# Pre-norm roots applied behind the projections, and attention one head deeper, in a hybrid decoder kernel

## The chip, the cores and the metric

One core of a Trainium2 chip runs the whole program. The metric is the device time of one execution in microseconds (us), lower is better. Engines are written as in the profile: PE (TensorE), DVE (VectorE), ACT (ScalarE), POOL (GpSimd), SP (the queue that issues most DMAs).

## The reference, cut to what matters

Tokens: T = 272 rows (16 learned meta tokens ahead of 256 real ones), model width 1024. Two layers.

```
layer 0: h += rms(rglru_block(rms(h, a_pre)), a_post)          # "ao" is the second norm
         h += rms(swiglu(rms(h, f_pre)), f_post)               # "f" is the first norm, "fo" the second
shared:  u = rms(h, kv_norm); ckv, k_rope = split(u @ w_dkv, [256])
         kv = rms(ckv, latent) @ w_ukv ; k_rope = rope(k_rope)
layer 1: cq = rms(rms(h, b_pre) @ w_dq, q_norm)                # kv_norm and b_pre share one root, "b"
         q = cq @ w_uq ; 16 heads: softmax(q k^T) v, causal, blocks of 128 queries
         h += rms(o @ w_o, b_post)                             # "bo"
         h += rms(moe_swiglu(rms(h, m_pre)), m_post)           # 8 experts, top 2
rms(x, g) = x * rsqrt(mean(x*x) + eps) * g
```

The root of a row is one number per token. It commutes with the matrix product over the features: rms(h, g) @ W = (h * g) @ W, each token's column then multiplied by its 1/root.

## The kernel before, in words

Activations lie transposed: a tile is 128 features by 272 tokens, and the residual hT has KD = 8 such blocks. Every product is formed from values split in two halves (hi is the rounded value, lo the rest), as three matmuls (`product`, L426 to L430): hi·hi, hi·lo, lo·hi. A tile of eight blocks is therefore 24 matmuls of 272 columns (`columns_tile`).

**Weights.** SP loads them in chunks of 128x2048 in the order of `PLAN`, RAW = 6 buffers deep. ACT rounds each to w_hi (L977), DVE subtracts to w_lo (L1331); both go to one of SPLIT = 3 buffers, so chunk n may only be rounded when PE has finished chunk n - 3. `ahead(n)` stands in ACT's and DVE's programs where they are to bring the chunks up to n.

**Tiles.** The PSUM tiles take six banks in the order of `tile_plan`; a tile's bank is free when its emptier, "A" (ACT) or "V" (DVE), has emptied the tile six places before. Banks 6 and 7 take the sums of squares.

**A norm** (`root`, `reciprocal_of_root`, `residual`, `squares`, `sum_taken`, `normalise`). For "ao" and "fo" ACT writes each emptied tile and its square, POOL adds six of the squares (`add_squares`, L890), PE multiplies by ones for the sum over partitions (L456, L449), ACT takes the root, DVE its reciprocal (1.85 us) and then, per block, scales mix (L1345) and adds it to hT (L1371). For the next norm, "f" or "b", ACT squares hT block by block (L997), PE sums all eight squares (L449, two matmul records each), ACT takes the root (L1004), DVE the reciprocal (L1340); then DVE writes the scaled block (L1345), ACT rounds it (L1011), DVE subtracts (L1359), and PE may use block k.

**Feed-forward.** 12 rounds j of gate tiles f_g and up tiles f_u, two each. ACT empties f_g with Silu, DVE multiplies f_u from PSUM by it into f_h; ACT and DVE split f_h into hid_hi and hid_lo. Then 8 f_down tiles.

**Latents.** PE runs ckv (2 tiles), krope (1), cq (3); ACT empties them with their squares; roots "ckv" and "cq"; then `ukv` gives keys and values: ACT empties kn and v tiles, POOL copies the rotary part of the keys to all heads (L907 to L909), fills `blank` with zeros and writes it out 34 times.

**Attention.** In PE's order, for head h: `scores(h)`; after heads 1, 5 and 9 the four tiles of the next group of queries; `turn_probs(h - LAG)` (transposes, L585); `weigh(h - LAG - 1)` (L595 to L598). DVE empties scores with the mask (L1562), ACT exponentiates (L1199), DVE divides (L1575), ACT copies the turned tile (L1211), and after heads 3, 7, 11 and 15 both split another weight chunk. LAG = 2. The output of each pair of heads is split by ACT (L1215) and DVE (L1583), and b_out (8 tiles) consumes it. The experts' loop follows.

Of the kernel before, what the change touches and what calls it, by code (L numbers as in the profile page):

```python
# [44 lines left out]
LAG = 2  # L45
# [22 lines left out]
def chunk_plan():  # L68
# [9 lines left out]
    plan += [("dkv", 0, KD * LORA), ("dkr", 0, KD * ROPE), ("dq", 0, KD * 256), ("dq", 1, KD * 128)]  # L78
# [9 lines left out]
EC = 4 * UT + KE // 2  # L88
assert EC % RAW == 0 and EC % SPLIT == 0

# [4 lines left out]
def tile_plan():  # L95
# [8 lines left out]
    for j in range(KF // 2):  # L104
        plan += [("f_g", 2 * j, "A"), ("f_g", 2 * j + 1, "A"), ("f_u", 2 * j, "V"), ("f_u", 2 * j + 1, "V")]
    plan += [("f_down", m, "A") for m in range(KD)] + [("ckv", m, "A") for m in range(KL)] + [("krope", 0, "V")]
    plan += [("cq", m, "A") for m in range(KQ)]
# [4 lines left out]
    plan += queries(0)  # L112
    for h in range(HEADS):
        plan += [("s", h, "V")]
        if h % 4 == 1 and h // 4 < 3:
            plan += queries(h // 4 + 1)
        if h >= LAG:
            plan += [("pt", h - LAG, "A")]
# [18 lines left out]
NORMED = {name: n - KD for name, n in PART.items()}  # L137
# [10 lines left out]
ADDED = {"ao": KD - 2, "fo": 2 * (KD - 2), "bo": 3 * (KD - 2)}  # L148
# [11 lines left out]
def pieces(name, k, src, dst):  # L160

    if name == "dkr":
        s = src[:, 0:k * ROPE].rearrange("p (k n) -> p k n", k=k)
        d = dst[:, 0:k * 3 * ROPE].rearrange("p (k n) -> p k n", k=k)
        h = ROPE // 2
        return [(d[:, :, 0:h], s[:, :, h:ROPE]), (d[:, :, h:ROPE], s[:, :, 0:h]),
# [20 lines left out]
def yoco_kernel(nc, w, params, consts, gain_rows, x_tok, out):  # L187
    with ExitStack() as ctx:
# [75 lines left out]
        s_sb = mix.rearrange("p k n -> p (k n)")[:, 0:3 * SW].rearrange("p (h n) -> p h n", h=3)  # L264
# [51 lines left out]
        sq_added = sem("sq_added")  # L316
        gated, gelu_done = sem("gated"), sem("gelu_done")
# [22 lines left out]
        nbias, rsum, rcp = (small[:, 112 + 16 * k:112 + 16 * k + 9] for k in range(3))  # L340
# [15 lines left out]
        def source(name, j):  # L356
# [10 lines left out]
                "dkr": lambda: w_dkv[:, :, LORA:LORA + ROPE],  # L367
                "dq": lambda: w_dq[:, :, 256 * j:min(256 * j + 256, QLORA)],
# [9 lines left out]
        def split_views(n, buf):  # L378
# [3 lines left out]
            cols = {"dkr": KD * 3 * ROPE, "uq": KQ * 512}.get(name, cols)  # L382
# [18 lines left out]
        def _(pe):  # L401
# [115 lines left out]
            pe.wait_ge(in_const, 16)  # L517
            sum_taken("f")
            for j in range(KF // 2):
                for name, key in (("f_g", "f_gate"), ("f_u", "f_up")):  # L520
                    wc = chunk(key, j)
                    for m in (2 * j, 2 * j + 1):
                        columns_tile(name, m, wc, P * (m % 2), u, KD, P, *([("chunk", CH[(key, j)])] if m % 2 else []),
                                     need="f" if (name, m) == ("f_g", 0) else None)
# [18 lines left out]

            sum_taken("b")
            wc = chunk("dkv", 0)
            for m in range(KL):
                columns_tile("ckv", m, wc, P * m, u, KD, P, *([("chunk", CH[("dkv", 0)])] if m else []),
                             need=None if m else "kv")
            columns_tile("krope", 0, chunk("dkr", 0), 0, u, KD, QK, ("chunk", CH[("dkr", 0)]))
            for m in range(KQ):  # L550
                columns_tile("cq", m, chunk("dq", m // 2), P * (m % 2), (ub_hi, ub_lo), KD, P,
                             *([("chunk", CH[("dq", m // 2)])] if m else []), need=None if m else "b", at=REAL)
                if m == 0:
                    for k in range(KL):
                        sum_emptied("ckv", "ckv", k, sq[:, k, :])
# [1249 lines left out]
```

## Time and profile before

| | |
|---|---|
| median of 3 runs | 1584.25 us (1583.27 to 1586.55) |
| the profiled execution's own time | 1584.72 us |
| its span, first to last instruction | 1582.9 us, so 1.8 us lie around it |
| PE busy | 1485.3 us (94%) |
| DVE busy | 1183.3 us (75%) |
| ACT busy | 1026.8 us (65%) |
| POOL busy | 95.6 us (6%) |
| mean granted TensorE clock | 0.976 of full |

Busy times of different engines overlap. PE's busy time counts a slow matmul as busy as a fast one, so the granted clock is to be read beside it.

### The profile page before, as it was taken

What the parts mean: (1) busy time and instruction counts of PE and PEld (TensorE: products, weight loads), DVE (VectorE), ACT (ScalarE), POOL (GpSimd) and SP (SyncE); (2) the same over time, 40 slices, a digit from 0 to 9 for tenths busy, and PEclk for the clock granted to TensorE, in tenths of its full rate; (3) what the DMA queues carried; (4) which work ended last, traced back from release to release, by engine and by line L of the source; (5) the groups of instructions that cost most, each with busy time, mean ns of one, the idle gap of its engine ahead of it and who ended that gap; (6) DMA issues with size and microseconds to landing.
All of it is one profiled execution on the core that took longest, in us unless ns stands there. A gap on an engine that the chain in (4) does not pass through costs nothing.

```text
span 1582.9 us, 21443 instructions
## 1 busy us (share of the span) xinstructions
PE 1485.3 (94%) x7852; PEld 1258.5 (80%) x7852; DVE 1183.3 (75%) x1089; ACT 1026.8 (65%) x1085; POOL 95.6 (6%) x112
## 2 busy tenths in 40 slices
PE   7787999997788879999999999999999999999997
PEld 6787999996676768877878878887887887887785
DVE  6685554535746278888888888888888888888987
ACT  6874444443565357777777767777767777767675
POOL 2001000000250110000000000000000000002500
PEclk9999999998899979999999999999999999999999
DMA  8345455542286259999999999999999999999993
GB/s 268 115 124 189 150 170 187 164 146 83 84 324 260 80 207 368 360 343 403 346 350 399 353 346 397 360 352 383 366 355 370 373 356 370 355 372 361 401 363 148
DMA packets 166704, 455.27 MB, mean 288 GB/s; under 512 B 8688, under 2 KB 77552, under 8 KB 152320
## 3 DMA queue, kind: packets, MB, share of 16 engines
q1 hardware_dynamic: 160432, 432.07, 75.5%
q0 software_dynamic: 6224, 22.55, 3.7%
q8 instruction: 32, 0.52, 0.1%
q14 instruction: 16, 0.13, 0.0%
HBM read 429.42 MB, written 25.17 MB: 287 GB/s over the span
## 4 chain that ended last, share of the span: by engine, by line
PE 84%; DVE 8%; ACT 4%; issue 3%; DMA 0%; DVEq 0%; SPq 0%; ACTq 0%
PE bank L428 26%; PE bank L430 26%; PE bank L429 26%; PE bank L698 2%; DVE w_lo L1593 1%; DVE w_lo L1331 1%; DVE x_lo L1683 1%; ACT w_hi L977 1%; ACT w_hi L1228 1%; PE bank L449 1%; DVE mix_sq L1345 1%; DVE rstd L1340 1%; PE bank L474 1%; PE bank L575 1%; PE bank L687 0%
## 5 line engine op out<-in xcount | busy, mean ns | idle before, releaser
L1593 DVE TENSOR_TENSOR w_lo<-raw,w_hi 128x2048 fp32r<-128x2048 f32 x338 | 774.4, 2302 | 139.8 <-ACT w_hi L1228 139.1
L1228 ACT CAST w_hi<-raw 128x2048 fp32r<-128x2048 f32 x338 | 645.6, 1916 | 261.7 <-PE bank L430 255.6
L428 PE MATMUL bank<-w_hi,x_hi 128*128 128x512 f32 x896 | 357.5, 399 | 3.6 <-DVE x_lo L1683 3.6
L429 PE MATMUL bank<-w_lo,x_hi 128*128 128x512 f32 x896 | 355.2, 396 | 0.0
L430 PE MATMUL bank<-w_hi,x_lo 128*128 128x512 f32 x896 | 354.9, 396 | 0.0
L1331 DVE TENSOR_TENSOR w_lo<-raw,w_hi 128x2048 fp32r<-128x2048 f32 (+8 forms) x93 | 153.1, 1669 | 163.7 <-ACT w_hi L977 163.6
L428 PE MATMUL bank<-u_hi,w_hi 128*128 128x272 f32 (+2 forms) x632 | 187.5, 297 | 19.1 <-DVE u_lo L1359 8.7
L428 PEld LDWEIGHTS bank<-w_hi,x_hi 128*128 128x128 f32 x896 | 169.0, 189 | 44.8 <-issue 3.8
L430 PEld LDWEIGHTS bank<-w_hi,x_lo 128*128 128x128 f32 x896 | 168.7, 188 | 41.2
L429 PEld LDWEIGHTS bank<-w_lo,x_hi 128*128 128x128 f32 x896 | 168.8, 188 | 39.5
L430 PE MATMUL bank<-u_hi,w_lo 128*128 128x272 f32 (+2 forms) x632 | 184.9, 293 | 0.0
L429 PE MATMUL bank<-u_lo,w_hi 128*128 128x272 f32 (+2 forms) x632 | 184.7, 292 | 0.0
L428 PE MATMUL bank<-w_hi,eh_hi 128*128 128x512 f32 x448 | 180.4, 403 | 1.3 <-DVE w_lo L1593 1.3
L430 PE MATMUL bank<-w_hi,eh_lo 128*128 128x512 f32 x448 | 177.6, 396 | 0.0
L429 PE MATMUL bank<-w_lo,eh_hi 128*128 128x512 f32 x448 | 177.4, 396 | 0.0
L977 ACT CAST w_hi<-raw 128x2048 fp32r<-128x2048 f32 (+8 forms) x93 | 124.9, 1372 | 65.2 <-PE bank L430 64.5
L428 PEld LDWEIGHTS bank<-u_hi,w_hi 128*128 128x128 f32 (+1 forms) x632 | 121.8, 193 | 22.6 <-issue 9.7
L429 PEld LDWEIGHTS bank<-u_lo,w_hi 128*128 128x128 f32 (+1 forms) x632 | 122.5, 194 | 0.0
L430 PEld LDWEIGHTS bank<-u_hi,w_lo 128*128 128x128 f32 (+1 forms) x632 | 122.2, 193 | 0.0
L428 PEld LDWEIGHTS bank<-w_hi,eh_hi 128*128 128x128 f32 x448 | 84.5, 189 | 23.9 <-DVE w_lo L1593 4.8
L430 PEld LDWEIGHTS bank<-w_hi,eh_lo 128*128 128x128 f32 x448 | 84.4, 188 | 20.5
L429 PEld LDWEIGHTS bank<-w_lo,eh_hi 128*128 128x128 f32 x448 | 84.5, 189 | 19.1
(271 smaller groups left out, 1513.5 us busy)
## 6 DMA issues: line engine op xcount, KB each, us to landing
raw<-in_m_w_gate_up SPq DMA_DIRECT2D x226, 1024.0 KB, 6.5
raw<-in_m_w_down SPq DMA_DIRECT2D x112, 1024.0 KB, 6.1
raw<-in_f_w_gate_up SPq DMA_DIRECT2D x24, 1024.0 KB, 5.2
raw<-in_f_w_down SPq DMA_DIRECT2D x12, 1024.0 KB, 5.2
raw<-in_a_w_in SPq DMA_DIRECT2D x10, 1024.0 KB, 7.7
x_slots<-mix_sq POOLq DMA_DIRECT2D x17, 512.0 KB, 17.0
y_slots<-mix_sq POOLq DMA_DIRECT2D x17, 512.0 KB, 17.9
raw<-in_a_w_out SPq DMA_DIRECT2D x8, 640.0 KB, 4.6
```

The source lines that it names most:

```text
L428: nc.tensor.matmul(o, a[0], b[0], start=start, stop=False)
L429: nc.tensor.matmul(o, a[0], b[1], start=False, stop=False)
L430: return nc.tensor.matmul(o, a[1], b[0], start=False, stop=stop)
L449: last = nc.tensor.matmul(ps[:, WIDE.get(name, ALL)], ones, src, start=(k == 0), stop=(k == kn - 1))
L474: last = nc.tensor.transpose(ps[:, t0:t0 + n], src[0:n, b, c * P:(c + 1) * P], ident[0:n, 0:n])
L575: last = nc.tensor.matmul(ps[:, c:c + kn], qT[h // 4 % 2][:, h % 4, P * b:P * b + P], kT[:, h, k0:k0 + kn], start=True, stop=True)
L698: last = nc.tensor.transpose(banks[6 + j % 2][:, P * f:P * f + P], e_h[:, j % 2, bass.ds(f, P, step=4)], ident)
L977: last = nc.scalar.copy(d, s)
L1228: nc.scalar.copy(w_hi[(NC0 + c) % SPLIT][:], raw[slot][:]).then_inc(hi_done, 1)
L1331: last = nc.vector.tensor_tensor(d, s, h, ALU.subtract)
L1340: link(nc.vector.reciprocal(rstd[:, i % 2, c], rstd[:, i % 2, c]))
L1593: nc.vector.tensor_tensor(w_lo[s][:], raw[(NC0 + c) % RAW][:], w_hi[s][:].bitcast(F32), ALU.subtract)\
```

## The change

1. In "f" and "b" the blocks h*g are split without the root (`split_blocks` on ACT, `residual_split` on DVE), inside the loop that adds the residual. PE goes block by block over four tiles at once (`blocks_outside`), and DVE multiplies each tile by 1/root as it leaves PSUM. The squares of hT are added by POOL, and PE sums two blocks instead of eight.
2. DVE now empties f_g, ckv and cq too; Silu runs from SBUF; the product of gate and up is a third DVE instruction.
3. The rotary key columns share a chunk with the last query columns ("dqr", two DMAs on one buffer); krope comes after cq, gets 1/root by one more small multiply, and its `krope_done` comes after the latent's normalise.
4. LAG = 3 with four score buffers; group 1 of the queries is projected before head 0 (two tiles) and right behind it (two tiles) instead of after head 1.

```diff
-LAG = 2
+LAG = 3
-    plan += [("dkv", 0, KD * LORA), ("dkr", 0, KD * ROPE), ("dq", 0, KD * 256), ("dq", 1, KD * 128)]
+    plan += [("dkv", 0, KD * LORA), ("dq", 0, KD * 256), ("dqr", 0, KD * (P + ROPE))]
...
             def sum_taken(name):
-                for k in range(KD):
-                    pe.wait_ge(sq_ready, SQ[name] + k + 1)
-                    sum_block(name, sq[:, k, :], k)
+                sum_added(name)
+                pe.wait_ge(sq_ready, SQ[name] + KD)
+                sum_block(name, sq[:, KD - 1, :], KD - 1)
...
+            def blocks_outside(tiles):
+                ps = [bank_of(name, m) for name, m, _, _, _, _, _, _ in tiles]
+                for k in range(KD):
+                    for o, (name, m, wc, c0, act, at, ready, keys) in zip(ps, tiles):
+                        pe.wait_ge(act_lo, ready(k))
+                        last = product(o[:, at], [x[:, k, c0:c0 + P] for x in wc], [x[:, k, at] for x in act],
+                                       k == 0, k == KD - 1)
+                        if k == KD - 1:
+                            mark(last, ("tile", TN[(name, m)]), *keys)
...
             queries(0)
+            queries(1, (0, 1))
             for h in range(HEADS):
...
                 scores(h)
-                if h % 4 == 1 and g < 3:
+                if h == 0:
+                    queries(1, (2, 3))
+                if h % 4 == 1 and 1 <= g < 3:
                     queries(g + 1)
...
-            add_squares("ao", "a_out")
-            add_squares("fo", "f_down")
+            add_squares("ao", lambda m: (emptied["A"], EMPTIED[TN[("a_out", m)]]))
+            add_squares("f", lambda m: (sq_ready, SQ["f"] + m + 1))
+            add_squares("fo", lambda m: (emptied["A"], EMPTIED[TN[("f_down", m)]]))
+            add_squares("b", lambda m: (sq_ready, SQ["b"] + m + 1))
...
+            def split_blocks(parts, after, n):
+                for k in range(KD):
+                    act.wait_ge(after, n + k + 1)
+                    for hi, gain, at in parts:
+                        nc.scalar.activation(hi[:, k, at], hT[:, k, at], ACT.Copy, scale=pr(gain, k)).then_inc(act_hi, 1)
+                    nc.scalar.activation(sq[:, k, :], hT[:, k, :], ACT.Square).then_inc(sq_ready, 1)
...
             root("ao")
-            squares(res_done, RES["ao"])
+            ahead(CH[("f_gate", 1)])
+            split_blocks([(u_hi, "f_pre", ALL)], res_done, RES["ao"])
             root("f")
-            rounded("f", u_hi, sq, KD)
+            ahead(CH[("f_up", 1)])
             prime(ACT.Silu)
...
             root("fo")
-            squares(res_done, RES["fo"])
+            ahead(CH[("dqr", 0)])
+            split_blocks([(u_hi, "kv_norm", ALL), (ub_hi, "b_pre", REAL)], res_done, RES["fo"])
             root("b")
...
+            ahead(CH[("ukv", 0)])
+            for n, (src, part) in enumerate([(ckv[:, k, :], ALL) for k in range(KL)] +
+                                          [(cq[:, k, REAL], REAL) for k in range(KQ)]):
+                if n == KL + 2:
+                    ahead(CH[("ukv", 1)])
+                act.wait_ge(emptied["V"], EMPTIED[TN[("ckv", 0)]] + n)
+                nc.scalar.activation(sq[:, n, part], src, ACT.Square).then_inc(latent_sq, 1)
+            root("ckv")
+            rounded("ckv", ckv_hi, ckv, KL)
+            act.wait_ge(krope_done, 1)
             root("cq")
             prime(ACT.Exp)
-            rounded("ckv", ckv_hi, ckv, KL)
             rounded("cq", cq_hi, cq, KQ, REAL)
...
+            def residual_split(name, gain, parts, n):
+                r = reciprocal_of_root(name)
+                for k in range(KD + 2):
+                    if k < KD:
+                        scaled_at(mix, mix, gain, k, r, ALL).then_inc(res_scaled, 1)
+                    if 1 <= k <= KD:
+                        dve.wait_ge(res_scaled, RES[name] + k)
+                        nc.vector.tensor_tensor(hT[:, k - 1, :], hT[:, k - 1, :], mix[:, k - 1, :], ALU.add)\
+                            .then_inc(res_done, 1)
+                    if k >= 2:
+                        for i, (lo, hi, g, at) in enumerate(parts):
+                            dve.wait_ge(act_hi, n + len(parts) * (k - 2) + i + 1)
+                            nc.vector.scalar_tensor_tensor(out=lo[:, k - 2, at], in0=hT[:, k - 2, at], scalar=pr(g, k - 2),
+                                                           in1=hi[:, k - 2, at].bitcast(F32), op0=ALU.mult,
+                                                           op1=ALU.subtract).then_inc(act_lo, 1)
...
             for j in range(KF // 2):
                 ahead(CH[("f_gate", j)] + 2)
+                for m in (2 * j, 2 * j + 1):
+                    ps = at_tile(dve, "f_g", m)
+                    if m >= 2:
+                        dve.wait_ge(f_h_done, m - 1)
+                    nc.vector.tensor_tensor(f_silu[:, m % 2, :], ps[:, 0:T], r, ALU.mult).then_inc(emptied["V"], 1)
                 ahead(CH[("f_up", j)] + 2)
                 for m in (2 * j, 2 * j + 1):
                     ps = at_tile(dve, "f_u", m)
...
+                    nc.vector.tensor_tensor(f_h[:, m % 4, :], ps[:, 0:T], r, ALU.mult).then_inc(emptied["V"], 1)
+                for m in (2 * j, 2 * j + 1):
+                    dve.wait_ge(f_silu_done, m + 1)
+                    dve.wait_ge(emptied["V"], EMPTIED[TN[("f_u", m)]])
+                    nc.vector.tensor_tensor(f_h[:, m % 4, :], f_h[:, m % 4, :], f_silu[:, m % 2, :], ALU.mult)\
+                        .then_inc(f_h_done, 1)
...
+            for m in range(KL):
+                ps = at_tile(dve, "ckv", m)
+                nc.vector.tensor_tensor(ckv[:, m, :], ps[:, 0:T], r, ALU.mult).then_inc(emptied["V"], 1)
+            for m in range(2):
+                ps = at_tile(dve, "cq", m)
+                nc.vector.tensor_tensor(cq[:, m, REAL], ps[:, REAL], r[:, REAL], ALU.mult).then_inc(emptied["V"], 1)
+            ahead(CH[("ukv", 0)])
...
+            normalise([("ckv", ckv_lo, ckv_hi, ckv, ckv, "latent", KL, ALL)], reciprocal_of_root("ckv"))
...
+            link(nc.vector.tensor_tensor(rope_a[NOPE:QK, :], rope_a[NOPE:QK, :], k_temp[NOPE:QK, :], ALU.add))
+            nc.vector.tensor_tensor(rope_a[NOPE:QK, :], rope_a[NOPE:QK, :], r[NOPE:QK, :], ALU.mult).then_inc(krope_done, 1)
+            ahead(CH[("ukv", 1)])
             normalise([("cq", cq_lo, cq_hi, cq, cq, "q_norm", KQ, REAL)], reciprocal_of_root("cq"))
```

## Rows read from the trace of the kernel before

**Rows 1.** Stretches: length; busy PE, PEld, DVE, ACT, POOL; PE clock; DMA share; GB/s.
```profile
143.50:157.85 14.35, 5.69 (x18) 3.95 (x17) 11.74 (x23) 5.58 (x13) 0.00 (x0) 0.88 0.24 77
171.97:376.30 204.33, 204.33 (x1634) 204.33 (x1633) 94.39 (x84) 85.27 (x99) 5.40 (x6) 1.00 0.52 169
376.30:392.64 16.34, 7.46 (x22) 4.91 (x21) 11.73 (x23) 6.27 (x15) 0.00 (x0) 0.79 0.01 2
392.64:427.66 35.02, 24.38 (x155) 22.42 (x155) 27.52 (x49) 18.63 (x39) 10.32 (x8) 0.85 0.28 88
431.02:445.27 14.25, 14.25 (x83) 12.62 (x83) 4.84 (x14) 13.89 (x33) 2.08 (x4) 1.00 0.37 125
450.65:525.58 74.93, 62.23 (x385) 49.34 (x385) 41.69 (x152) 40.89 (x113) 12.43 (x24) 0.93 0.72 272
580.00:1560.00 980.00, 976.60 (x4289) 783.38 (x4288) 840.20 (x501) 708.73 (x522) 32.56 (x11) 1.00 0.98 363
```

**Rows 2.** Timeline ahead of the feed-forward: start, duration, engine, line, operation.
```profile
144.06 1.85 DVE L1340 RECIPROCAL rstd<-rstd 128x272 f32<-128x272 f32 x1 [0.98 <-ACT rstd L1004]
145.95 0.92 DVE L1345 SCALAR_TENSOR_TENSOR mix_sq<-mix_sq,par,rstd 128x272 f32<-128x272 f32 x2
146.78 0.43 DVE L1371 TENSOR_TENSOR hT<-hT,mix_sq 128x272 f32<-128x272 f32 x1
147.55 0.44 DVE L1371 TENSOR_TENSOR hT<-hT,mix_sq 128x272 f32<-128x272 f32 x1
147.82 5.68 PE L449 MATMUL bank<-mix_sq,con 128*128 128x272 f32 x16 [4.32 <-ACT mix_sq L997]
```

**Rows 3.** Busy time of two stretches of equal length at either clock.
```profile
158.00:161.00 3.00, 3.00 (x13) 2.80 (x14) 3.00 (x9) 1.67 (x4) 0.00 (x0) 0.50 0.02 5
162.00:165.00 3.00, 3.00 (x26) 3.00 (x25) 0.26 (x2) 2.99 (x4) 0.00 (x0) 1.00 0.00 0
```

**Rows 4.** POOL's adds of squares (ns min/median/max), and one beside a DVE split.
```profile
L890 POOL TENSOR_TENSOR mix_sq<-mix_sq x18: 730/776/1802, 120.3 to 545.6; 128x272 f32<-128x272 f32 x12, 128x256 f32<-128x256 f32 x6
533.09 2.29 DVE L1331 TENSOR_TENSOR w_lo<-raw,w_hi 128x2048 fp32r<-128x2048 f32 x1 [7.56 <-ACT w_hi L977]
534.18 1.80 POOL L890 TENSOR_TENSOR mix_sq<-mix_sq 128x256 f32<-128x256 f32 x1 [2.09 <-ACT mix_sq L991]
```

**Rows 5.** Timeline of ACT in the feed-forward: one split of a chunk.
```profile
178.39 1.89 ACT L977 CAST w_hi<-raw 128x2048 fp32r<-128x2048 f32 x1
```

**Rows 6.** Timeline of the latents and behind them.
```profile
378.50 1.85 DVE L1340 RECIPROCAL rstd<-rstd 128x272 f32<-128x272 f32 x1 [5.67 <-ACT rstd L1004]
409.09 2.50 DVE L1331 TENSOR_TENSOR w_lo<-raw,w_hi 128x512 fp32r<-128x512 f32 x4
417.67 6.29 DVE L1331 TENSOR_TENSOR w_lo<-raw,w_hi 128x512 fp32r<-128x512 f32 x4 [6.08 <-ACT w_hi L977]
417.89 2.43 POOL L907 COPY kT<-rope_a 32x2304 f32<-32x2304 f32 x1 [10.02 <-PE bank L430]
429.82 1.20 ACT L1011 CAST cq_hi<-cq 128x256 fp32r<-128x256 f32 x3 [2.69 <-DVE cq L1345]
```

**Rows 7.** Timeline of PE in attention: the scores of heads 5, 7, 8 and 15.
```profile
468.60 1.00 PE L575 MATMUL bank<-kT,qT_odd 96*128 96x144 f32 x4
478.69 1.00 PE L575 MATMUL bank<-kT,qT_odd 96*128 96x144 f32 x4
481.29 1.00 PE L575 MATMUL bank<-kT,qT_even 96*128 96x144 f32 x4
508.49 1.00 PE L575 MATMUL bank<-kT,qT_odd 96*128 96x144 f32 x4
```

**Rows 8.** Waits between 450 and 522 us (in total, times, longest), and the one behind attention.
```profile
PE bank L585 <- DVE mix_sq L1575: 5.9, 5, 2.3
PE bank L595 <- ACT mix_sq L1211: 4.5, 4, 2.0
525.58 0.38 PE L428 MATMUL bank<-u_hi,w_hi 128*128 128x256 f32 x1 [2.25 <-DVE u_lo L1583]
```

More of the change, by code:

```diff
@@ L88, with landings @@
 EC = 4 * UT + KE // 2
+PAIRED = CH[("dqr", 0)]
+def landings(n):
+    return n // RAW + 1 + (n >= PAIRED and n % RAW == PAIRED % RAW)
 assert EC % RAW == 0 and EC % SPLIT == 0
@@ L104, in tile_plan @@
     for j in range(KF // 2):
-        plan += [("f_g", 2 * j, "A"), ("f_g", 2 * j + 1, "A"), ("f_u", 2 * j, "V"), ("f_u", 2 * j + 1, "V")]
-    plan += [("f_down", m, "A") for m in range(KD)] + [("ckv", m, "A") for m in range(KL)] + [("krope", 0, "V")]
-    plan += [("cq", m, "A") for m in range(KQ)]
+        plan += [("f_g", 2 * j, "V"), ("f_g", 2 * j + 1, "V"), ("f_u", 2 * j, "V"), ("f_u", 2 * j + 1, "V")]
+    plan += [("f_down", m, "A") for m in range(KD)] + [("ckv", m, "V") for m in range(KL)]
+    plan += [("cq", m, "V") for m in range(KQ)] + [("krope", 0, "V")]
     for half in range(2):
@@ L135 @@
 PART = {name: sum(k for _, k in PARTS[:i]) for i, (name, _) in enumerate(PARTS)}
-NORMED = {name: n - KD for name, n in PART.items()}
+NORMED = {name: n - PART["ckv"] for name, n in PART.items()}
 WIDE = {"cq": REAL, "bo": REAL}
@@ L517, in _ @@
             pe.wait_ge(in_const, 16)
+            def blocks_outside(tiles):
[7 more added lines that the diff above has]
+                            mark(last, ("tile", TN[(name, m)]), *keys)
+            wg, wu = chunk("f_gate", 0), chunk("f_up", 0)
+            blocks_outside([(name, m, wc, P * m, u, ALL, lambda k: PART["f"] + k + 1,
+                             [("chunk", CH[(key, 0)])] if m else [])
+                            for name, key, wc in (("f_g", "f_gate", wg), ("f_u", "f_up", wu)) for m in range(2)])
             sum_taken("f")
-            for j in range(KF // 2):
+            for j in range(1, KF // 2):
                 for name, key in (("f_g", "f_gate"), ("f_u", "f_up")):
@@ L542, in _ @@
             sum_emptied("fo", "f_down", KD - 1, sq[:, KD - 1, :])
-            sum_taken("b")
[L545 to L555, printed above, removed]
+            ub = (ub_hi, ub_lo)
+            wk, wq = chunk("dkv", 0), chunk("dq", 0)
+            blocks_outside([("ckv", m, wk, P * m, u, ALL, lambda k: PART["kv"] + 2 * k + 1,
+                             [("chunk", CH[("dkv", 0)])] if m else []) for m in range(KL)] +
+                           [("cq", m, wq, P * m, ub, REAL, lambda k: PART["kv"] + 2 * k + 2,
+                             [("chunk", CH[("dq", 0)])] if m else []) for m in range(2)])
+            sum_taken("b")
+            (q_hi, r_hi), (q_lo, r_lo) = chunk("dqr", 0)
+            columns_tile("cq", 2, (q_hi, q_lo), 0, ub, KD, P, at=REAL)
+            columns_tile("krope", 0, (r_hi, r_lo), 0, u, KD, QK, ("chunk", CH[("dqr", 0)]))
+            for k in range(KL):
+                pe.wait_ge(latent_sq, k + 1)
+                sum_block("ckv", sq[:, k, :], k)
             for k in range(KQ):
-                sum_emptied("cq", "cq", k, sq[:, KL + k, REAL])
+                pe.wait_ge(latent_sq, KL + k + 1)
+                sum_block("cq", sq[:, KL + k, REAL], k)
             pe.wait_ge(act_lo, PART["ckv"] + KL)
@@ L1481, in _ @@
                 ahead(CH[("a_out", m)] + 2)
-            residual("ao", "a_post")
-            normalise([("f", u_lo, u_hi, sq, hT, "f_pre", KD, ALL)], reciprocal_of_root("f"))
+            residual_split("ao", "a_post", [(u_lo, u_hi, "f_pre", ALL)], PART["f"])
+            ahead(CH[("f_gate", 1)])
+            r = reciprocal_of_root("f")
             def f_low(m):
```

118 lines of the change are left out of this document (57 added, 61 removed).

## Prediction

> **What bounds the kernel now.** I first cut the span into stretches and read PE's column [rows 1]. From 580 us on, in the experts' loop, PE is busy for 976.6 of 980 us at full clock; from 171.97 to 376.30 us, in the feed-forward, for all of it. The change has nothing to give in either. What is left are three places where PE waits: the norm ahead of the feed-forward (busy 5.7 of 14.4 us), the norm ahead of the latents and the latents themselves (7.5 of 16.3 and 24.4 of 35.0 us), and attention (62.2 of 74.9 us). In all three the granted clock is below 1, so part of the busy time is also slow time.
>
> Next the timeline of the first norm [rows 2]. A reciprocal ends at 145.91 us, DVE scales and adds a block every 0.77 us, PE sums the squares from 147.82 for 5.7 us, then a root and a second reciprocal (1.85 us) pass before the first product at 157.85 us, where a stretch of rows 1 ends. Only the second half, sum, root and reciprocal, stands between a ready hT and PE. After such a pause PE starts at the lower level, 1.2 GHz: 13 matmuls in 3 us against 26 at 2.4 GHz [rows 3], so 0.23 against 0.124 us for 272 columns including the next load, and a start that is slow for about 3.4 us loses some 1.6 us of PE work.
>
> Last, the waits of attention. A head costs PE 2.60 us when nothing is late [rows 7]; PE waits for DVE's division (5.9 us in 5 waits) and for ACT's copy of the turned tile (4.5 us in 4), and 2.25 us more for the last split of the attention output [rows 8].
>
> I work on the clock of the profile before and carry what each place saves.
>
> **First norm and feed-forward.** The residual loop gets a third DVE instruction per block. Scale to add takes 0.41 us, add to scale 0.35, the new subtraction like a scale 0.41: 1.17 us per block. The first low half comes in the third turn, at 145.95 + 0.41 + 0.41 + 0.35 + 0.41 + 0.37, and ends near 148.4 us. There PE starts, 9.4 us earlier than before. ACT has rounded f_gate 1 in the shadow of the reciprocal (1.9 us, 144.0 to 145.9), so its first block isn't late; per block it needs two instructions of 0.43 us and keeps up.
>
> PE needs 12 matmuls of 0.124 = 1.49 us per block, 11.9 for eight. It pauses from 143.5 us on as before, so the first 2.9 us or so run at 1.2 GHz and lose 1.3. It is through at 148.4 + 11.9 + 1.3 = 161.6 us, unless DVE is slower.
>
> That is the one new load I weigh. The six adds of squares now run on POOL beside DVE's loop. An add takes 0.78 us, 1.8 us when it meets a DVE split of 2.3 us; it then ended 0.6 us after the split [rows 4]. The other way round, DVE's four pieces of a split that take 2.50 us alone took 6.29 beside POOL's copies [rows 6], 3.8 us for three copies. So an instruction of either waits out one of the other. No row shows POOL adds between short DVE instructions: the cost to DVE is 0 if POOL always yields, at most one whole slow add of 1.2 us each if it never does (half of the 2.4 us copy that blocked a piece). I take 0.7, nearest to the 0.78 of a lone add: 6 x 0.7 = 4.2 us a loop. The last low half, 155.85 us without, comes at 160.05; PE needs it at 161.6 - 1.5 = 160.1. So here it costs nothing, with no margin; at 1.2 each it costs 3 us. The Trainium skill ("SBUF — State Buffer", Who interferes with whom) has the rule that a DVE instruction with two SBUF inputs and a GpSimd instruction that reads SBUF exclude each other for a whole instruction. All three of the loop's instructions are of that kind; by that rule, with each add at its full 0.78, the loop would be 4.7 us longer and this place would give 0.5 us less.
>
> After the last product two sums follow (0.75 us) and f_g 2 starts at 162.35 us instead of 171.97. **Saved: 9.6 us.** Nothing gives it back at once: root, reciprocal and two multiplies free bank 0 by 165.7, f_up 1 is split by 168.0, and PE asks for both at 162.35 + 5.95 = 168.3.
>
> In each later round DVE does four more instructions of 0.44 us (about 1.7 us), and empties f_g in place of ACT. The chain of one round is: multiply, Silu, ACT's split 1.9 [rows 5], DVE's 2.3 [rows 4], two multiplies, two products, two low halves, the next split on DVE 2.3: 10.5 us against PE's 204.33 us for 12 rounds and f_down, of which a round takes 96 x 0.1253 = 12.03. With 1.5 us to spare it stays hidden behind PE's products; a chain longer than PE's round would cost 12 times the excess.
>
> **Second norm and latents.** The same loop with two subtractions: 0.41 x 3 + 0.35 = 1.57 us per block from 380.4 us. Without POOL the last low half ends at 393.05; with 4.2 us for the adds at 397.25. PE starts at 382.85, starts slow and is by its own work ready at 396.3; with DVE's pace it ends at 397.25 + 0.75 = 398.0. Then in order: DVE splits dqr (2.7 us) to 400.05; reciprocal of "b" to 401.95; four multiplies to 403.5; ukv 0 (2.5) to 406.0; cq 2 at 406.4; ACT's square and root "ckv" at 407.4; reciprocal, scales and halves to 411.1, when PE begins the keys (before 427.66).
>
> But PE soon waits for its six banks, as ACT empties keys only behind cq's rounding. That chain decides: krope's four small instructions (1.8 us) to 412.9; ukv 1 on DVE, 2.50 us alone, 6.29 beside the three POOL copies that krope_done releases at the same moment [rows 6]. I take 6.29, since it is the same chunk beside the same copies: 419.2; reciprocal 421.0; ACT has cq rounded at 422.7, before 431.02 (429.82 + 1.20 [rows 6]). From there ACT works without a pause for 14.25 us, busy 13.9 [rows 1], and does so again: 437.0. PE's queries end at 438.8 and, after the rotation (2.2 us), scores start at 441.1 instead of 450.65. The two tiles of group 1 fill those 2.2 us, in which PE was idle. **Saved: 9.6 us.** The table load for Exp, 1.5 us, lies beside DVE's split; SP issues one short DMA more, for a chunk that is loaded during f_down, long before its use.
>
> **Attention.** From the start of scores to those of head 5 before: 468.60 - 450.65 = 17.95 us. After: head 0, two query tiles, rotation until 5.2 us; DVE empties and divides a head in about 1.35; the third ends at 9.3; ACT exponentiates head 3, splits uq 2 (1.75) and only then copies the first turned tile, at 11.9; weigh 1.2: head 5 at 13.1. Saved 4.9 (2.15 of it the two tiles done earlier). From head 5 to 15, ten heads at 2.60 and two query groups at 4.3 are 34.6 us; before it took 508.49 - 468.60 = 39.9 [rows 7]. A third head between scores and turning is 2.6 us more for the division, so the DVE waits there (0.41, 0.40, 1.24 and 0.28) go. The waits for ACT's copy (1.04 and 1.19) stay: copy and weigh both move by a head, and ACT's split still stands ahead of the copy. Saved 39.9 - 36.8 = 3.1. From head 15's scores to the last block of the output: before 525.58 - 508.49 = 17.1; after 0.84 + 9.9 to the last weigh, then ACT's split of b_out 2, DVE's, and the last low half, 14.4: saved 2.7. With a shorter wait there, PE should run at full clock into b_out; I count half of the 1.4 us: 0.7. The weight loads and the 34 zero writes start earlier with everything else. **Saved: 4.9 + 3.1 + 2.7 + 0.7 = 11.4 us, less 0.1 of rounding, 11.3.**
>
> **Sum.** 9.6 + 9.6 + 11.3 = 30.5 us, from the profiled execution's 1584.72: 1554.2. That execution was 0.5 us above the median of the runs, so 1554 for the median.
>
> **Rivals.**
> - POOL's adds hold DVE up by the upper bound, 1.2 us each: 3 us lost in each norm (the loop then sets PE's pace in both), 1554 + 6 = 1560. For it speaks that all of DVE's instructions read two SBUF operands; against, that a lone add is 0.78. Chance 0.2.
> - POOL yields: adds cost nothing and ukv 1 takes 2.50. The latents end 1.7 + 3.8 us earlier: 1554 - 5.5 = 1548.5. Against it stands the 6.29. Chance 0.12.
> - Attention gives half: the depth moves waits only, because ACT is the late one and its splits stay ahead of the copies; the first heads wait as long as before. 1554 + 5.5 = 1559.5. For it speak 4.5 us of waits on ACT [rows 8]. Chance 0.15.
> - The other side: the feed-forward's chain gets longer than PE's round. DVE and ACT hand over four times a round instead of three; if a round took 12.03 + 2.5 us, 12 x 2.5 = 30 us would eat everything, more makes the kernel slower. From 10.5 us that takes 4 us more per round than the rows give, on engines that are busy 94 and 85 of 204 us [rows 1]. At that point 1584, at 1 us more 1596. Chance 0.02.
> - The change does nothing, because the second root was never what PE waited for: excluded in the first norm by rows 2, so 1584 has 0.01.
>
> **Numbers.** My forecast has the remaining 0.5. Its own uncertainty is some 3 us; upwards the first and third rival reach 1560 and together 1565, downwards the second 1548.5 and, with all of the clock's gain, 1546. Range 1546 to 1565. A change within 0.2% (3 us, about what a measurement of this kernel can tell) has 0.02, slower 0.02, faster 0.96.
>
> **What would show it.** Right: first product of the feed-forward near 148.4 us at 1.2 GHz, f_g 2 near 162.4, no PE wait from there to the end of f_down; DVE's loop at about 1.8 us per block ahead of the feed-forward and 2.1 ahead of the latents where POOL adds; ukv 1's split above 6 us beside L907's copies; scores 19 us earlier; PE waits on the division almost gone, those on ACT's copy still near 1 us each. Wrong: DVE's loop at twice its length, PE idle inside the gate and up tiles, or attention still about 75 us long.

## The result and the profile after

The changed kernel takes 1564.35 us (median of 4 runs, 1559.83 to 1565.19), the kernel before in the same session 1584.28: a ratio of 0.9863, 95% interval 0.9852 to 0.9875. A second set of four runs gave 1563.69 (1560.28 to 1564.47); over all eight the median is 1563.8, which the experiments below are held against. So some 20.5 us went, where the forecast said 30.5; the time lies inside the range of 1546 to 1565, close to its upper end. The profiled execution took 1564.89 us, its span is 1563.1 against 1582.9: 19.8 us less.

The stretches of the changed kernel that answer to [rows 1], with the same columns:

```profile
149.41:163.55 14.14, 14.14 (x101) 14.02 (x101) 12.34 (x19) 5.38 (x13) 5.53 (x6) 0.90 0.05 10
374.89:392.00 17.11, 16.91 (x109) 16.40 (x110) 15.83 (x34) 9.27 (x23) 8.37 (x11) 0.82 0.01 2
402.47:434.56 32.09, 26.85 (x138) 24.39 (x139) 18.75 (x34) 19.51 (x45) 14.06 (x19) 0.80 0.47 163
434.56:503.03 68.47, 57.62 (x367) 46.34 (x367) 41.70 (x152) 40.60 (x111) 11.46 (x22) 0.95 0.77 293
525.58:550.00 24.42, 16.11 (x78) 15.94 (x79) 20.71 (x67) 12.33 (x22) 4.13 (x5) 0.55 0.40 143
556.05:562.00 5.95, 5.95 (x14) 4.69 (x15) 2.29 (x1) 0.44 (x2) 0.00 (x0) 0.50 0.41 120
575.00:1545.00 970.00, 967.03 (x4240) 775.24 (x4238) 834.56 (x506) 702.11 (x518) 33.79 (x11) 1.00 0.98 363
```

In both norms PE is now busy while DVE still applies the residual (14.14 of 14.14 and 16.91 of 17.11 us). Attention lasts 68.47 us instead of 74.93. The last line is the experts' loop, untouched. The two lines above it are the surprise: the routing runs at a clock of 0.55, and the loop's first 5.95 us at 0.50, with 14 matmuls.

The first norm, and the product behind the sums (answers to [rows 2, 4]):

```profile
144.93 1.85 DVE L1388 RECIPROCAL rstd<-rstd 128x272 f32<-128x272 f32 x1 [0.98 <-ACT rstd L1052]
148.76 0.50 DVE L1423 SCALAR_TENSOR_TENSOR u_lo<-hT,par,u_hi 128x272 fp32r<-128x272 f32 x1
149.41 0.57 PE L442 MATMUL bank<-u_hi,w_hi 128*128 128x272 f32 x1 [5.04 <-DVE u_lo L1423]
149.80 0.85 POOL L928 TENSOR_TENSOR mix_sq<-mix_sq 128x272 f32<-128x272 f32 x1 [8.98 <-ACT mix_sq L1045]
149.94 1.01 DVE L1423 SCALAR_TENSOR_TENSOR u_lo<-hT,par,u_hi 128x272 fp32r<-128x272 f32 x1
163.29 0.62 PE L463 MATMUL bank<-mix_sq,con 128*128 128x272 f32 x2
163.55 0.49 PE L442 MATMUL bank<-u_hi,w_hi 128*128 128x272 f32 x1
```

The same subtraction takes 0.50 us alone and 1.01 us when a POOL add began just before it; it ends 0.3 us behind the add. The six adds of the loop cost DVE 0.51 us (four times) or 0.58 us (twice, on the residual's add), 3.2 us in all.

The latents and the start of attention (answers to [rows 6]):

```profile
404.29 6.30 DVE L1379 TENSOR_TENSOR w_lo<-raw,w_hi 128x512 fp32r<-128x512 f32 x4
404.38 2.56 POOL L947 COPY kT<-rope_a 32x2304 f32<-32x2304 f32 x1 [13.18 <-PE bank L444]
412.81 1.20 ACT L1059 CAST cq_hi<-cq 128x256 fp32r<-128x256 f32 x3 [6.53 <-DVE cq L1393]
416.41 0.80 PE L442 MATMUL bank<-w_hi,ckv_hi 128*128 128x512 f32 x1 [5.05 <-ACT kT L1218]
434.56 0.97 PE L605 MATMUL bank<-kT,qT_even 96*128 96x144 f32 x4 [0.20 <-issue]
```

PE's waits from 400 to 560 us (in total, times, longest), and the one behind attention (answers to [rows 8]):

```profile
PE bank L625 <- ACT mix_sq L1259: 9.0, 5, 3.2
PE bank L442 <- ACT kT L1218: 5.0, 1, 5.0
PE bank L615 <- DVE mix_sq L1658: 1.4, 1, 1.4
503.03 0.38 PE L442 MATMUL bank<-u_hi,w_hi 128*128 128x256 f32 x1 [0.47 <-DVE u_lo L1666]
```

The division is waited for once (1.4 us) instead of five times (5.9), ACT's copy of the turned tile for 9.0 us instead of 4.5. The longest is the first weighing, and ACT's timeline shows what stands ahead of that copy:

```profile
444.07 1.73 ACT L1017 CAST w_hi<-raw 128x768 fp32r<-128x768 f32 x4
445.82 0.59 ACT L1259 COPY mix_sq<-bank 128x512 f32<-128x512 f32 x1
446.46 1.11 PE L625 MATMUL bank<-mix_sq,v_tok 128*64 128x256 f32 x2 [3.25 <-ACT mix_sq L1259]
```

How far the changed execution is ahead of the one before, at points that both have:

| point | before | after | ahead |
|---|---|---|---|
| first reciprocal, ahead of all that changed | 144.06 | 144.93 | -0.9 |
| f_g 2 | 171.97 | 163.55 | 8.4 |
| cq rounded | 431.02 | 414.01 | 17.0 |
| first scores | 450.65 | 434.56 | 16.1 |
| head 5's scores | 468.60 | 448.78 | 19.8 |
| head 15's scores | 508.49 | 488.91 | 19.6 |
| b_out, last block begins | 525.58 | 503.03 | 22.5 |
| b_out summed | 549.15 | 525.10 | 24.1 |
| experts' loop begins | 579.55 | 556.05 | 23.5 |
| its first transposes of e_h | 605.02 | 584.18 | 20.8 |
| its last, in expert 8 | 1529.52 | 1509.73 | 19.8 |

Two things have to be explained: 24.1 us at most were gained and not 30.5, and 4.3 of them are gone at the end.

### The profile page after: what moved, and what is told of

Same layout as the page of the kernel before. It is cut to its first block, busy times and chain, and to the rows that moved or that the text cites. A ratio compares the mean times of both kernels' runs of the same rounds, so it can differ in the third digit from the quotient of the medians.

```text
span 1563.1 us, 21470 instructions
## 1 busy us (share of the span) xinstructions
PE 1480.1 (95%) x7828; PEld 1257.7 (80%) x7828; DVE 1201.0 (77%) x1119; ACT 1026.3 (66%) x1080; POOL 106.6 (7%) x124
## 3 DMA queue, kind: packets, MB, share of 16 engines
HBM read 429.42 MB, written 25.17 MB: 291 GB/s over the span
## 4 chain that ended last, share of the span: by engine, by line
PE 85%; DVE 8%; ACT 4%; issue 2%; DMA 0%; DVEq 0%; SPq 0%; ACTq 0%
PE bank L442 27%; PE bank L444 26%; PE bank L443 26%; PE bank L732 2%; DVE w_lo L1676 2%; DVE w_lo L1379 1%; DVE x_lo L1766 1%; ACT w_hi L1276 1%; ACT w_hi L1017 1%; DVE rstd L1388 1%; PE bank L488 1%; PE bank L605 1%; DVE mix_sq L1393 1%; PE bank L625 0%; PE bank L721 0%
## 5 line engine op out<-in xcount | busy, mean ns | idle before, releaser
L443 PEld LDWEIGHTS bank<-w_lo,x_hi 128*128 128x128 f32 x896 | 169.9, 190 | 39.9
L444 PEld LDWEIGHTS bank<-w_hi,eh_lo 128*128 128x128 f32 x448 | 84.4, 188 | 20.5
```

Source lines behind the costliest of these rows:

```text
L443: nc.tensor.matmul(o, a[0], b[1], start=False, stop=False)
L444: return nc.tensor.matmul(o, a[1], b[0], start=False, stop=stop)
```

## The experiments

All ran against the kernel before; "against the changed kernel" is the difference of medians to 1563.8. The spread of its eight runs is 5.4 us, and the kernel before had medians of 1584.3 to 1585.8 beside them, so a difference under 1.5 us says little by itself and the trace has to carry it. S is the start of the first scores. Two of the expectations, of depth2 and of group1_back, reckon with head 5's scores at S + 14.9; the row stands at 448.78 us, S + 14.2.

**Depth alone taken back (depth2).**

```diff
-LAG = 3
+LAG = 2
```

> The changed kernel with the softmax of two heads in flight again instead of three, nothing else undone. My theory: depth is what removed the waits for the division (5.9 us over 5 before, none after), so they come back at heads 8 to 16 and the attention takes 3 to 5 us longer (scores of head 5 to scores of head 15 again about 42 us instead of 39.5): about 1568. Rival (the third head in flight gave nothing here, since the wait only changed from the division to ScalarE's copy of the turned probabilities, which stands at 1.1 to 2.1 us five times after the change): no change, 1563 to 1565, with waits of the same sum on another releaser.

Measured: 1568.15 us (4 runs, 1565.11 to 1569.71), ratio 0.9891 [0.9874, 0.9908], 4.4 us slower than the changed kernel. PE's waits in attention:

```profile
PE bank L615 <- DVE mix_sq L1658: 5.9, 5, 2.3
PE bank L625 <- ACT mix_sq L1259: 4.8, 5, 2.0
```

The 5.9 us in 5 waits of [rows 8] are back to the digit. From the first scores to b_out's last block it takes 72.12 us (433.99 to 506.11) instead of 68.47. The theory holds: the third head is what took these waits away. Where the time comes back isn't as expected. From head 5's to head 15's scores it takes 39.9 us, not 42; the changed kernel's profile above has 40.1. The tail, from head 15's scores to b_out's last block, takes 17.8 us instead of 14.1: a wait of 1.56 us on the last division stands there, and one of 1.64 us instead of 0.47 ahead of that block.

**The second query group back behind head 1 (group1_back).**

```diff
-            queries(1, (0, 1))
             for h in range(HEADS):
...
-                if h == 0:
-                    queries(1, (2, 3))
-                if h % 4 == 1 and 1 <= g < 3:
+                if h % 4 == 1 and g < 3:
```

and the same on ScalarE, VectorE and in the order of the tiles.

> The changed kernel with the second group of queries projected behind head 1 again. My theory: the 4.9 us that the forecast gave to the start of the attention (head 5 at S + 13.1 instead of S + 18.0) came out as 3.1 (S + 14.9), so S + 18 comes back, where S is the start of the first scores, but S itself is 1.3 us earlier, since the two projections ahead of it (q_nope 2 and 3, about 2.5 us at full clock) move behind it: 2 to 4 us slower in all, about 1567. Rival (the matrix work only moves; the granted clock of 0.50 to 0.74 at 444 to 452 us, which follows the wait of 3.25 us at the first weighing, takes all of it back): within 1 us of 1564.

Measured: 1567.3 us (1566.83 to 1569.45), ratio 0.9886 [0.987, 0.9903], 3.5 us slower. The size is as expected, one detail isn't: the scores do not start earlier. From the first product of the keys to the first scores it is 32.12 us (403.37 to 435.49), with the group in front 32.09. PE idles in front of the scores for 2.24 us again, waiting for the rotation: the two tiles had filled that gap for nothing.

**Both back (both_back).** The two diffs together.

> The changed kernel with both parts in the attention undone (two heads in flight, the second query group projected after head 1); the two norms and the latents stay as changed. One at a time they cost about 4.3 us (depth2) and 3.5 us (group1_back). My theory: they cover different stretches (waits from head 5 on; the first five heads), so together they cost 7 to 8.5 us: 1570.5 to 1572.5, and the norms and latents are worth the other 13 to 14 us of 21. Rival (the forecast's size of 11.3 us for the attention is right and something else of the change is worth less): 1575. Rival (they cover the same waits): 1568.5.

Measured: 1571.63 us (5 runs, 1568.64 to 1572.99), ratio 0.9906 [0.9893, 0.9919], 7.8 us slower than the changed kernel. First scores to b_out's last block: 75.02 us, which is the 74.93 of [rows 1]. 4.4 + 3.5 = 7.9: the parts add up, and the attention was worth 7.8 us, not 11.3. The norms and latents gave the other 13, by subtraction; they were not taken back one by one.

**The sums back on PE (pe_sums).**

```diff
-                sum_added(name)
-                pe.wait_ge(sq_ready, SQ[name] + KD)
-                sum_block(name, sq[:, KD - 1, :], KD - 1)
+                for k in range(KD):
+                    pe.wait_ge(sq_ready, SQ[name] + k + 1)
+                    sum_block(name, sq[:, k, :], k)
...
-            add_squares("f", lambda m: (sq_ready, SQ["f"] + m + 1))
...
-            add_squares("b", lambda m: (sq_ready, SQ["b"] + m + 1))
```

> The changed kernel with GpSimd's additions of the squares for the two pre-norms (f and b) taken out: TensorE sums all eight blocks of squares itself behind the tiles, as before the change. The forecast priced these additions at 4.2 us in each of VectorE's two loops and thought the loop set the end. My theory now: TensorE is busy for 14.14 of 14.14 us in the first norm and 16.9 of 17.1 us in the second, so VectorE's loop is hidden and its additions cost nothing; six more sums of about 0.46 us each stand on TensorE's path in each norm: 2.8 us twice, 5 to 6 us slower than the changed kernel, about 1569.5. Rival (the additions do set the two loops, as forecast): 2 x (3.5 - 2.8) = 1.4 us faster or the same, 1562 to 1564.

Measured: 1566.81 us (1566.34 to 1567.53), ratio 0.9885 [0.987, 0.9901], 3.0 us slower. The sums of the first norm behind its 96 products:

```profile
163.38 3.83 PE L463 MATMUL bank<-mix_sq,con 128*128 128x272 f32 x16
```

3.83 us for eight blocks, against some 0.7 for the two sums at 162.83 of the changed kernel. By the first product of the keys this variant is 4.9 us behind the changed kernel (407.33 against 402.47), close to the 5 to 6 expected, but only 3.6 behind at the first scores (438.15) and 2.2 at b_out's last block (505.27). Behind the first scores its clock stood at 0.50 for 3.4 us (451.5 to 454.9), the changed kernel's for 6.8 (445.9 to 452.7). So the end is 3.0 us later and not 5 to 6. The rival is out: the adds hold DVE up, and DVE isn't what PE waits for there.

**GpSimd's key copies later (pool_late).**

```diff
             at(pool, "tile", TN[("cq", KQ - 1)])
+            pool.wait_ge(act_lo, PART["cq"] + KQ)
```

> The changed kernel with one wait more: GpSimd's three copies of the rotated key rows (2.56, 0.86, 2.35 us) start when the query latent is rounded, not beside VectorE's split of chunk ukv 1, which takes 6.30 us beside them where the same split of ukv 0 takes 2.49 alone. My theory: the query latent is rounded 3.8 us earlier (410.2 instead of 414.0), ScalarE's chain of 14.25 us behind it and the first scores move with it: 1560 to 1561. Rival (TensorE's own work from 402 to 434 us is the bound, or the copies now slow VectorE's splits of uq 0 and uq 1 and give it back): 1563 to 1565.

Measured: 1559.06 us (5 runs, 1558.0 to 1560.47), ratio 0.9838 [0.9824, 0.9851], 4.7 us faster than the changed kernel. Its split of ukv 1, PE's wait and the first scores:

```profile
404.86 2.50 DVE L1380 TENSOR_TENSOR w_lo<-raw,w_hi 128x512 fp32r<-128x512 f32 x4
413.18 0.51 PE L442 MATMUL bank<-w_hi,ckv_hi 128*128 128x512 f32 x1 [1.16 <-ACT kT L1219]
428.73 0.97 PE L605 MATMUL bank<-kT,qT_even 96*128 96x144 f32 x4
```

The split takes 2.50 instead of 6.30 us. The scores start at 428.73 against 434.56 us, which is 25.69 us behind the first product of the keys (403.04) instead of 32.09: 6.4 less. 3.8 come from the split, 2.6 are clock: with a wait of 1.16 instead of 5.05 us PE goes on at 1.00, where the changed kernel starts again at 0.50:

```profile
413.18:428.73 15.55, 15.42 (x102) 14.16 (x103) 9.00 (x19) 13.68 (x33) 9.46 (x14) 1.00 0.59 206
```

against, in the changed kernel,

```profile
416.41:434.56 18.15, 17.96 (x102) 16.39 (x103) 6.08 (x19) 13.99 (x33) 8.39 (x16) 0.85 0.65 230
```

the same 102 matmuls in 15.55 and in 18.15 us. GpSimd's copies now hold up VectorE's split of uq 0 instead (412.46 to 417.41 us, 4.95 us long, where it took 1.97 at 415.69), but PE waits for none of it.

**ScalarE's splits behind its copy (split_behind).** The two lines `if h % 4 == 3: ahead(...)` moved below the copy of the turned tile.

> The changed kernel with ScalarE's chunk splits of the attention (uq 2, uq 3, b_out 0) moved behind its copy of the turned probabilities in the same step. My theory: the wait of 3.25 us at the first weighing and those of 1.1 to 1.3 us at heads 7 and 11 are this split of 1.9 us ahead of the copy; moved, the first falls to about 1.4 and the other two go: 2 to 4 us faster than the changed kernel, 1560 to 1562. Rival (the later split is late for VectorE's subtraction and so for the next group's projection, or the copy waits for the weighing ahead of it anyway): 1564 or slower.

Measured: 1562.73 us (1562.64 to 1563.07), ratio 0.9859 [0.9843, 0.9875], 1.1 us faster, inside the changed kernel's own spread. The wait of 3.25 us is gone, but two new ones stand elsewhere:

```profile
463.11 0.38 PE L442 MATMUL bank<-cq_hi,w_hi 128*128 128x256 f32 x1 [0.88 <-DVE w_lo L1379]
481.49 1.12 PE L625 MATMUL bank<-mix_sq,v_tok 128*64 128x256 f32 x2 [3.05 <-ACT mix_sq L1257]
```

What the split no longer delays in its own step it delays in the next one, by way of DVE: ACT rounds the chunk from 475.09 to 476.99 us, DVE, which has stood idle for 2.67 us, takes its share at 477.02 and only then, at 479.23, empties the next scores, and ACT's exponentials wait 2.69 us for them. First scores to b_out: 67.58 us, against 68.47 in one execution of the unaltered changed kernel and 67.23 in another (next run). My theory was right about the cause of the 3.25 us and wrong about the gain.

**The changed kernel again (after_again).** No edit.

> The changed kernel itself, unaltered, as the reference of this call. Expected 1562 to 1566; it shows how far its runs lie apart, and whether the low clock at the start of the experts' loop comes in each of them.

Measured: 1563.69 us, ratio 0.9868 [0.9852, 0.9883]. The profiled one was by chance the shortest, 1560.28 us. The start of its experts' loop, to be read beside the line 556.05:562.00 of the result:

```profile
552.55:558.50 5.95, 5.95 (x19) 4.72 (x20) 2.19 (x1) 1.31 (x1) 0.00 (x0) 0.71 0.45 136
```

19 matmuls in 5.95 us where the other execution did 14. In attention both had 6.8 us at 0.50, at different places: here 440.6 to 444.0 and 491.8 to 495.2 us, in the other 445.9 to 452.7 in one piece. The first of the two stands just ahead of the first weighing, which then waits 1.93 us for ACT instead of 3.25, so it costs little; the other execution took 1.24 us more to b_out. One program, the same instructions: of the 4.8 us between the two spans 1.3 were there at the first reciprocal already, and the rest goes with where the low clock falls.

**Filling PE's gaps ahead of the experts' loop (fill, before_fill).**

```diff
+            def fill(n):
+                for _ in range(n):
+                    nc.tensor.matmul(banks[5][:, :], ones, con[:, 0:512], start=True, stop=True)
+
+            fill(8)
             pe.wait_ge(gw_done, 1)
...
             mark(last, "logits")
+            fill(10)
...
                     mark(last, ("first_x", k // 4))
+            fill(8)
```

The products go into a bank that nobody reads.

> The changed kernel with 26 matrix products of constants (128x512 each, into a bank nobody reads) put where TensorE waits between the end of the attention block's output projection and the experts' loop: 8 ahead of the residual, 10 behind the logits, 8 behind the first expert's token selection. They change no result. My theory: 22.6 us saved up to 503 us became 19.8 at the end because TensorE's granted clock was 0.50 from 530 to 562 us; the first 14 products of the experts' loop took 0.43 us each instead of 0.234 (2.7 us), and 4.9 us of products at 545 to 550 ran at half clock (up to 2.4 us). With the gaps filled the clock stays at 1.00 for part of it: 1559.5 to 1561.5, and the profile shows the loop's first products at 0.234 us. Rival (VectorE's chain and the weights' transfers set this stretch whatever TensorE's clock): 1563 to 1565.

> The kernel before with the same 26 products of constants in the same three places as in the run fill. My theory: what was given back after the attention is a matter of where TensorE's low clock falls; before the change the experts' loop began at full clock in the profiled run (its first products 0.234 us apart), so the filling gains at most 1 us here: 1583.5 to 1585. Rival (both kernels lose the same 2.7 us at the loop's start in most runs): 1581 to 1582.5, and then nothing was given back.

Measured: 1562.62 us (1562.08 to 1562.99) for the changed kernel with it, ratio 0.9859 [0.9842, 0.9875], 1.2 us faster; 1588.16 us (11 runs) for the kernel before with it, ratio 1.0018 [1.0009, 1.0027], 3.2 us slower. My price of a filling was wrong:

```profile
550.56 7.03 PE L672 MATMUL bank<-con 128*128 128x512 f32 x16
557.02 0.80 PE L442 MATMUL bank<-w_hi,x_hi 128*128 128x512 f32 x1
```

Eight of them are 16 passes and 7.03 us, 0.88 each at full clock, not 0.234; x_lo was there at 554.1 us, so the filling held the loop back by 2.9 us, and the ten behind the logits the positions by 2.1. The changed kernel won in spite of that.

**Filling that fits (fill_fit, before_fill_fit).** The same with 3, 5 and 4 products.

> The changed kernel with 3, 5 and 4 products of constants where the run fill had 8, 10 and 8. One such product took 0.88 us at full clock (two passes of 0.44), not the 0.234 us that I had reckoned with, so the ten behind the logits held the next step back by 2.1 us and the last eight held the experts' loop back by 2.9 us; twelve of 0.88 us fit into the waits of 3.48, 5.08 and 3.62 us. My theory: without that hold-back the full clock gives 3 to 5 us against the changed kernel: 1559 to 1561. Rival (so few products don't keep the clock up, which stays at 0.50 for part of 528 to 560 us): 1562 to 1564.

> The kernel before with the same 3, 5 and 4 products. If the changed kernel lost time after the attention through the clock and the kernel before did not, this gains clearly less than fill_fit does: 1583 to 1584.5 against 1585. If both lose the same, it gains the same 3 to 5 us, 1580 to 1582. The run before_fill was 3.2 us slower than before where fill was about 1 us faster than the changed kernel, which speaks for the first.

Measured: 1559.04 us (5 runs, 1557.17 to 1560.21), ratio 0.9831 [0.9819, 0.9844], 4.8 us faster than the changed kernel; the kernel before with it 1585.46 (12 runs, 1580.71 to 1588.03), ratio 0.9994 [0.9983, 1.0005], no difference in the median, 1 us above what I had expected. Four of its twelve runs, 1580.71 to 1580.91, lie below all 17 runs of the kernel before (1583.13 to 1588.08), so in some executions the filling helps there too. fill_fit at the loop's start:

```profile
549.86 3.60 PE L672 MATMUL bank<-con 128*128 128x512 f32 x8
553.70 0.49 PE L442 MATMUL bank<-w_hi,x_hi 128*128 128x512 f32 x1 [0.24 <-DVE x_lo L1773]
553.70:559.65 5.95, 5.95 (x25) 4.80 (x26) 3.07 (x2) 1.95 (x2) 0.00 (x0) 1.00 0.69 236
```

25 matmuls in 5.95 us, as in the kernel before, whose loop began at 1.00:

```profile
579.55:585.50 5.95, 5.95 (x25) 4.81 (x26) 2.85 (x2) 1.94 (x2) 0.00 (x0) 1.00 0.45 148
```

So what the changed kernel lost behind the attention was for the most part clock, and the kernel before, as a rule, did not lose it: the filling gives the one 4.8 us and the other, in the median, nothing.

**Together (best).** fill_fit, pool_late, and uq 2's split alone behind the copy.

```diff
-                if h % 4 == 3:
+                if h in (7, 11, 15):
                     ahead(CH[("uq", 0)] + h // 4 + 2)
...
+                if h == 3:
+                    ahead(CH[("uq", 0)] + 2)
```

> The changed kernel with three edits that the runs before point to: the 3, 5 and 4 products of constants of fill_fit, GpSimd's wait of pool_late, and ScalarE's split of uq 2 alone moved behind its copy of the turned probabilities (step 3; in the run split_behind this took away the wait of 3.25 us at the first weighing, while the splits at steps 7 and 11 moved behind the copy brought 0.88 and 3.05 us of new waits, so they stay in front). My theory: the three lie in different stretches and add up: 4.7 + 4.6 + 1 to 2 us under the changed kernel's 1563.7, 1552.5 to 1555. Rival (the sizes don't add, because the low clock falls somewhere else when the stretches move): 1556 to 1559.

Measured: 1557.02 us (5 runs, 1554.81 to 1559.3), ratio 0.9822 [0.9809, 0.9835]: 6.8 us under the changed kernel, 28.8 under the one before, the fastest of all, but short of the 1552.5 to 1555 that I expected and inside the rival's 1556 to 1559. Two waits of PE show in the trace. One is a slip of mine: the steps go on to 20, and my list leaves out step 19, where b_out 2 was split:

```profile
492.70 1.88 ACT L1025 CAST w_hi<-raw 128x2048 fp32r<-128x2048 f32 x1
497.30 0.57 PE L442 MATMUL bank<-u_hi,w_hi 128*128 128x256 f32 x1 [3.75 <-DVE u_lo L1676]
```

The split now comes behind a table load, the last low half waits behind DVE's share of it, and PE stands for 3.75 us where it stood for 0.47. The other is the moved split itself: the first weighing waits 1.61 us instead of 3.25, but at 442.34 us PE now waits 1.42 us for the low half of uq 2, and the two together are 3.03. What the sum would be without the slip was not measured, and the rival, that the sizes don't add because the low clock falls elsewhere, is not excluded.

## Why the prediction was 10 us short

The two profiled spans are 19.8 us apart where the forecast has 30.5. The 10.7 us between are 0.9 lost ahead of the change, 0.3 in the first norm, 1.9 in the latents, 3.3 in the attention and 4.3 behind it:

- **First norm, 9.6: right.** Measured 8.4; 0.9 was lost ahead of anything that the change touches, so 9.3 by itself. PE starts at 149.41 (148.4 + 0.9 = 149.3) at the lower clock. The adds cost DVE 0.51 to 0.58 each where I took 0.7, and nothing on the path, as forecast; the first rival (1.2 each) and the second (POOL yields) are both out by the 1.01. Two readings of mine were off and cost nothing: by the forecast's own intervals the last low half ends at 155.4 us without the adds, not at 155.85, so there was some margin; and the wait of 0.28 us that it lists among DVE's is one on ACT. The Trainium skill ("SBUF — State Buffer", Who interferes with whom) says that the two exclude each other for a whole instruction. The trace agrees: the subtraction that began 0.14 us behind an add ended 0.3 us behind its end. The price was less than a whole add, 0.51 to 0.58 us for one of 0.85 to 1.01.
- **Feed-forward hidden: right.** There is no wait of PE from 163.55 us to the end of f_down.
- **Latents, 9.6: the mechanism right, 1.9 short.** cq was rounded 17.9 us earlier with the 0.9 taken off, exactly as forecast (9.6 + 8.3), ukv 1's split took 6.30 us beside the copies. But the scores came 17.0 earlier instead of 19.2 (0.3 of it from the first norm). I had let ACT's chain of 14.25 us set them; behind it PE resumed after a wait of 5.05 us at 0.50, where the same stretch of the kernel before ran at 1.00 [rows 1], and became the later one. pool_late shows it: take the wait away and the clock gives back 2.6 us beyond the 3.8.
- **Attention, 11.3: the step that failed by size.** The trace has 8.0 and both_back 7.8. To head 5: 14.2 us instead of 13.1, so 3.7 saved instead of 4.9. Head 5 to 15: 40.1 us instead of 36.8, so nothing saved instead of 3.1; the waits on the division went as forecast, but a new wait on ACT's copy (1.25 us at 485.08) joined the two of 1.13 and 1.28, 3.7 us where the forecast has 2.2, and PE ran at 0.50 until 452.7 us, nearly 2 us of lost work that the forecast had at nothing. The tail was right, 14.1 against the forecast 14.4; b_out gave 1.5 us instead of 0.7. In the second profile, with half of the low clock ahead of the first weighing and half in the tail, the three are 13.2, 38.3 and 15.7 us: the start as forecast, the heads 1.5 us over it through the third wait alone, and the tail 1.6 longer. The third rival, attention gives half, had a part of it right: ACT is the late one, its split stands ahead of the copy. But the depth did more than move waits, it gave 4.4 us (depth2).
- **The sum: a step that was missing.** I carried what each place saves to the end. At the end 4.3 us less arrived: 0.55 in residual and routing, 2.65 in the loop's first products at 0.50, 1.05 in the last expert. fill_fit, which only fills PE's waits, gets 4.8 us back, and the same filling gives the kernel before nothing in the median. The Trainium skill ("TensorE: Matmul & The Clock Gate", Part 1: The HAM clock gate) says that how many matmuls run slow varies from run to run of the same kernel. The two executions of the changed one, 4.6 us apart, agree. It also puts the ramp's penalty under 1% of a typical kernel's span. Here the 4.3 us are 0.3% of the span, but a fifth of the gain.

The 1.05 us in the last expert are clock too. Two groups of transposes of e_h lie 25.17 us apart there in the changed kernel and 23.62 before the change:

```profile
1493.58:1517.20 23.62, 23.62 (x104) 18.96 (x104) 21.44 (x13) 15.38 (x11) 0.97 (x1) 1.00 1.02 373
1472.26:1497.43 25.17, 25.17 (x105) 20.11 (x105) 21.54 (x13) 15.53 (x12) 0.98 (x1) 0.93 1.00 376
```

In all fourteen traces PE waits 1.8 to 2.3 us for DVE ahead of the first of the two. In nine of them a stretch at 0.50 follows (1473.3 to 1476.7 us in the changed kernel) and the distance is 25.1 to 25.2 us, in the other five it stays at 1.00 and the distance is 23.6. The full clock at the loop's start doesn't decide it: before_fill has that and still lost the 1.5 us here. The wait itself was 0.5 us longer in the kernel before (2.25 against 1.77), which leaves 1.05. Open is what decides whether the clock falls behind such a wait.

The time came out inside the range, but partly by luck. The upper end of 1565 was the sum of two rivals; the first did not happen, the third did in part, and the 4.3 us of clock behind the attention stood in neither.

## What to carry to other kernels

A saving ahead of a stretch with short waits isn't simply carried through it: shifting the work also shifts where TensorE's low clock falls, so check the clock of the first products behind each wait, not only the waits. Where several engines meet at one semaphore, look for what it releases on the engine that holds another one up, as GpSimd's copies do VectorE's split (6.30 us instead of 2.50); one wait on GpSimd, worth 4.7 us, was more than half of the whole attention part. And a pipeline made one stage deeper removes the wait of the late engine only; the next one, here ScalarE with its split ahead of its copy, takes over part of it.

## What the runs showed that I had not expected

- A product of plain f32 constants, 128x512, takes 0.88 us at full clock in two passes, where the kernel's rounded operands take 0.234 us. The norms' sums are of the same kind (3.83 us for 16 passes over 272 columns, two per block, where a product takes 0.124), which is why six adds on an otherwise idle engine pay.
- Twelve such products that change no result, 10.6 us of extra PE work in 12.2 us of waits, made a kernel of 1564 us 4.8 us faster.
- The first weighing waits for ACT 3.25 us in one execution of the changed kernel and 1.93 in another, where the low clock fell just ahead of it; the four behind it agree to 0.01 us.
